# A streaming encoder trunk with mixture-of-experts layers: pairs of 1 MB weight chunks fetched in one 2 MB transfer

## What is computed

```
h = h + concat(chunk_band_attention(q, k, v), multiscale_pool(p)) @ w_out_even    # layer 0 mixer
h = h + hierarchical_moe(rms_norm(h))                                             # layer 0 experts
h = h + concat(spatial_gating(u, vv), stick_breaking_attention(q, k, v)) @ w_out_odd
h = h + hierarchical_moe(rms_norm(h))
# hierarchical_moe: each token takes 1 of 4 groups and 2 of its 8 experts;
# 32 experts, each with w_gate, w_up [1024, 256] and w_down [256, 1024]
```

## Time and profile before

| What | Value |
|---|---|
| Three runs | 591.1, 592.69, 593.89 us; median 592.69 |
| Span of the profiled execution, first to last instruction | 590.9 us |
| PE busy | 542.0 us, 92% of the span |
| DVE, ACT, POOL busy | 182.4, 180.0, 6.5 us |
| Read from memory | 234.45 MB, 399 GB/s over the span |
| SP's queue (q1) | 33328 packets, 232.07 MB, 95.2% of 16 DMA engines |
| Chain that ended last | PE 72%, DMA 21%, ACT 4%, DVE 2% |

### The profile page before, as it was taken

One profiled execution on the slowest core, in us unless ns is written; L12 is line 12 of the kernel. 1 busy time (PEld: TensorE's weight loads), 2 busy tenths in 40 slices (PEclk: granted clock), 3 DMA queues, 4 the chain that ended last, 5 costly groups with the idle time before them and its releaser, 6 DMA issues.

```text
span 590.9 us, 9379 instructions
## 1 busy us (share of the span) xinstructions
PE 542.0 (92%) x3978; PEld 339.6 (57%) x3978; DVE 182.4 (31%) x311; ACT 180.0 (30%) x341; POOL 6.5 (1%) x16
## 2 busy tenths in 40 slices
PE   6999999999999998768799999999999999986786
PEld 5788787555546544142488878875555455451533
DVE  4687845311101100010365466543111011010102
ACT  5745835111111111010384696541110111110101
POOL 0000000000000000000000000000000000000000
PEclk8999999999999999797889999999999999998979
DMA  8999999999999999999999984698999999999996
GB/s 322 421 422 419 421 420 419 422 420 422 419 419 420 420 420 422 420 421 416 420 419 420 421 361 168 262 423 349 424 420 420 420 420 422 419 420 420 421 416 240
DMA packets 34098, 236.20 MB, mean 400 GB/s; under 512 B 3777, under 2 KB 4801, under 8 KB 6017
## 3 DMA queue, kind: packets, MB, share of 16 engines
q1 hardware_dynamic: 33328, 232.07, 95.2%
q0 software_dynamic: 720, 3.45, 1.4%
HBM read 234.45 MB, written 1.05 MB: 399 GB/s over the span
## 4 chain that ended last, share of the span: by engine, by line
PE 72%; DMA 21%; ACT 4%; DVE 2%; issue 1%; SPq 0%; ACTq 0%
PE psum L1317 15%; DMA raw<-stream 15%; PE psum L1296 9%; PE psum L1345 8%; PE psum L1373 8%; PE psum L265 8%; PE psum L266 8%; PE psum L267 8%; DMA late<-stream 5%; PE psum L1388 1%; DMA xT<-x_turned 1%; ACT hid L1458 1%; PE psum L1354 1%; PE psum L523 1%; ACT whi L250 1%
## 5 line engine op out<-in xcount | busy, mean ns | idle before, releaser
L1317 PE MATMUL psum<-raw,x 128*32 128x512 f32 x680 | 91.4, 639 | 20.6 <-issue 12.0
L257 DVE TENSOR_TENSOR raw_lo<-raw,whi 128x1024 fp32r<-128x1024 f32 x52 | 62.4, 1222 | 40.8 <-ACT whi L250 40.8
L1296 PEld LDWEIGHTS psum<-pick,h 128*128 128x128 f32 x512 | 60.2, 196 | 17.3 <-issue 15.1
L1373 PE MATMUL psum<-y,pickT 128*128 128x256 f32 x256 | 69.3, 403 | 0.0
L1296 PE MATMUL psum<-pick,h 128*128 128x128 f32 x512 | 64.0, 283 | 1.0 <-DVE pick L1260 1.0
L265 PE MATMUL psum<-whi,hnT_hi 128*128 128x512 f32 x144 | 58.5, 406 | 6.0 <-DVE hnT_lo L369 3.4
L1373 PEld LDWEIGHTS psum<-y,pickT 128*128 128x128 f32 x256 | 45.5, 193 | 31.5 <-issue 27.1
L250 ACT CAST whi<-raw 128x1024 fp32r<-128x1024 f32 x52 | 53.0, 1047 | 34.2 <-PE psum L267 28.6
L1268 DVE TENSOR_TENSOR pick<-pick,lists 128x256 f32<-128x256 f32 x16 | 6.8, 425 | 179.8 <-PE psum L1388 179.8
L266 PE MATMUL psum<-whi,hnT_lo 128*128 128x512 f32 x144 | 58.0, 403 | 0.0
L267 PE MATMUL psum<-raw_lo,hnT_hi 128*128 128x512 f32 x144 | 57.8, 402 | 0.0
(11 more groups left out here) (213 smaller groups left out, 502.2 us busy)
## 6 DMA issues: line engine op xcount, KB each, us to landing
raw<-stream SPq DMA_DIRECT2D x157, 1024.0 KB, 26.7
late<-stream SPq DMA_DIRECT2D x60, 1024.0 KB, 23.0
raw<-stream SPq DMA_DIRECT2D x2, 512.0 KB, 5.6
xT<-x_turned SPq DMA_DIRECT2D x2, 512.0 KB, 6.7
h<-x SPq DMA_DIRECT2D x1, 1024.0 KB, 11.5
pb<-even_bias POOLq DMA_DIRECT2D x1, 1024.0 KB, 14.0
pool_c<-even_pool POOLq DMA_DIRECT2D x1, 1024.0 KB, 9.5
out<-h SPq DMA_DIRECT2D x4, 256.0 KB, 2.2
```

The source lines that it names most:

```text
L257: nc.vector.tensor_tensor(raw_lo[PLACE[c][0]][:, cols], chunk(c)[:, cols], whi[:, n % SPLIT, cols].bitcast(F32), ALU.subtract).then_inc(lo ...
L1296: mm = nc.tensor.matmul(psum[:, b, (k - ks[0]) * P:(k - ks[0] + 1) * P], h[:, t, k * P:(k + 1) * P], pick[:, t, :], start=(t == 0), stop=( ...
L1317: nc.tensor.matmul(psum[rows, b, :], lhs[:, rows], chunk(c)[:, e * W4:(e + 1) * W4], start=start, stop=stop).then_inc(moe_used, 1)
L1373: nc.tensor.matmul(psum[:, 4 + i, t * QUARTER:(t + 1) * QUARTER], pickT[:, t * P:(t + 1) * P], y[:, i % 2, :], start=(q == 0 and t == 0), ...
```

## The change

In the stretches named below as alone, chunks come one by one as before. Elsewhere two neighbouring chunks (an even number and the next) come in one transfer of 2 MB into two neighbouring places, and one semaphore tells of both. In memory `stream` is laid out anew: for each pair of chunks and each partition, 16 KB together; a chunk that comes alone is read with 8 KB out of each 16 KB. Alone are chunks 0 to 3, 16 to 45, 104 to 109, 126 to 155 and 214 to 217 (74 chunks); 72 pairs remain: 4 to 15, 46 to 103, 110 to 125 and 156 to 213. A pair waits for both of its places. The choice of places is made over pairs of places (0,1), (2,3) ... (14,15), (17,18) ... (23,24); place 16 stays single. In the spill path, four transfers take the place of two.

```diff
+DOUBLES = tuple((p, p + 1) for p in itertools.chain(range(0, RAW, 2), range(RAW + 1, PLACES, 2)))
+ALONE = frozenset(itertools.chain(range(0, 4), range(16, 46), range(104, 110), range(126, 156), range(214, CHUNKS)))
+def transfers():
+    found, c = [], 0
+    while c < CHUNKS:
+        together = (c,) if c in ALONE else (c, c + 1)
+        found.append(together)
+        c += len(together)
+    return tuple(found)
...
-        place = min(open_to, key=lambda p: (free[p], p))
...
+        fitting = [(p,) for p in open_to] if len(chunks) == 1 else [d for d in DOUBLES if set(d) <= set(open_to)]
+        chosen = min(fitting, key=lambda ps: (max(free[p] for p in ps), ps))
...
-        raw = [fixed(f"raw{i}", [P, CH]) for i in range(RAW)]
+        raw = [fixed(f"raw{i}", [P, 2, CH]) for i in range(RAW // 2)]
...
-        late = [at(f"late{n}", [P, CH], kib) for n, kib in enumerate(range(10, 82, 8))]
+        late_alone = at("late_alone", [P, CH], 10)
+        late = [at(f"late{n}", [P, 2, CH], kib) for n, kib in enumerate(range(18, 82, 16))]
...
+        def from_stream(c):
+            return stream[c // 2, :, c % 2, :]
...
-            sp.dma_start(chunk(c), stream[c]).then_inc(landed[place], 16)
...
+        def load_chunks(sp, chunks):
+            for c in chunks:
+                place_free(sp, c)
+            c = chunks[0]
+            if len(chunks) == 1:
+                sp.dma_start(chunk(c), from_stream(c)).then_inc(landed[PLACE[c].told_by], 16)
+            else:
+                sp.dma_start(two_places(PLACE[c].place)[:], stream[c // 2]).then_inc(landed[PLACE[c].told_by], 16)
...
-            for c in range(2, CHUNKS):
-                if c == RAW + 3:
+            for chunks in TRANSFERS[2:]:
+                if chunks[0] == RAW + 3:
                     sp.wait_ge(ev.pool_c_landed, 16)
...
-        "stream": stream,
+        "stream": np.ascontiguousarray(stream.reshape(CHUNKS // 2, 2, P, CH).transpose(0, 2, 1, 3)),
```

More of the change, by code:

```diff
@@ L96 @@
               (OUT1 - 0.9, OUT1 + 1.1, OUT1 + 1.1, OUT1 + 0.5, OUT1 + 0.5, OUT1 + 2.1, OUT1 + 3.1))
+DOUBLES = tuple((p, p + 1) for p in itertools.chain(range(0, RAW, 2), range(RAW + 1, PLACES, 2)))
[7 more added lines that the diff above has]
+    return tuple(found)
+TRANSFERS = transfers()
+Placed = namedtuple("Placed", "place told_by nth leaves")
 def places():
-    found, free, inside = [], [-1] * PLACES, [[] for _ in range(PLACES)]
-    for c in range(CHUNKS):
+    found, free, inside, told = [], [-1] * PLACES, [[] for _ in range(PLACES)], [0] * PLACES
+    for chunks in TRANSFERS:
+        c = chunks[0]
         layer = int(c >= PROJ1)
@@ L110, in places @@
         open_to = [p for p in range(PLACES) if p < RAW or is_moe(c) and (p >= RAW + TILES_IN or not last_quad)]
-        place = min(open_to, key=lambda p: (free[p], p))
[L112 to L115, removed]
+        fitting = [(p,) for p in open_to] if len(chunks) == 1 else [d for d in DOUBLES if set(d) <= set(open_to)]
+        chosen = min(fitting, key=lambda ps: (max(free[p] for p in ps), ps))
+        for c, p in zip(chunks, chosen):
+            leaves = inside[p][-1] if inside[p] and free[p] == inside[p][-1] else None
+            found.append(Placed(p, chosen[0], told[chosen[0]], leaves))
+            inside[p].append(c)
+            free[p] = c
+        told[chosen[0]] += 1
     return found
 PLACE = places()
-BEHIND = min(c for c in range(CHUNKS) if MOE0 + SPILL_AT * PER_QUAD <= (PLACE[c][2] or 0) < PROJ1)
+BEHIND = min(cs[0] for cs in TRANSFERS for c in cs if MOE0 + SPILL_AT * PER_QUAD <= (PLACE[c].leaves or 0) < PROJ1)
 C_ID, C_NTRI, C_NONE, C_LT, C_IOTA, C_EPS, C_REV = 0, 128, 256, 384, 512, 545, 546
@@ L192, in hybrid_kernel, with two_places, place_free @@
         moe_used = sem("moe_used")
+        def two_places(place):
+            return raw[place // 2] if place < RAW else late[(place - RAW - 1) // 2]
         def chunk(c):
-            place = PLACE[c][0]
-            return raw[place][:] if place < RAW else late[place - RAW][:]
-        def chunk_landed(eng, c):
[L199 to L205, removed]
+            place = PLACE[c].place
+            if place == RAW:
+                return late_alone[:]
+            return two_places(place)[:, place % 2 if place < RAW else (place - RAW - 1) % 2, :]
+        def from_stream(c):
+            return stream[c // 2, :, c % 2, :]
+        def chunk_landed(eng, c):
+            eng.wait_ge(landed[PLACE[c].told_by], 16 * (PLACE[c].nth + 1))
+        def place_free(sp, c):
+            place, leaves = PLACE[c].place, PLACE[c].leaves
+            if leaves is None:
                 if place >= RAW:
                     late_free(sp, int(c >= PROJ1), place - RAW)
-            elif is_moe(before_it):
-                sp.wait_ge(moe_used, EACH * (moe_no(before_it) + 1))
-            else:
-                sp.wait_ge(w_used, 2 * mixer_no(before_it) + 2)
-            sp.dma_start(chunk(c), stream[c]).then_inc(landed[place], 16)
+            elif is_moe(leaves):
+                sp.wait_ge(moe_used, EACH * (moe_no(leaves) + 1))
+            else:
+                sp.wait_ge(w_used, 2 * mixer_no(leaves) + 2)
+        def load_chunks(sp, chunks):
+            for c in chunks:
+                place_free(sp, c)
+            c = chunks[0]
+            if len(chunks) == 1:
+                sp.dma_start(chunk(c), from_stream(c)).then_inc(landed[PLACE[c].told_by], 16)
+            else:
+                sp.dma_start(two_places(PLACE[c].place)[:], stream[c // 2]).then_inc(landed[PLACE[c].told_by], 16)
         def late_free(sp, layer, n):
@@ L256, in split_lo @@
                 dve.wait_ge(hi_done, 2 * n + part + 1)
-                nc.vector.tensor_tensor(raw_lo[PLACE[c][0]][:, cols], chunk(c)[:, cols],
+                nc.vector.tensor_tensor(raw_lo[PLACE[c].place][:, cols], chunk(c)[:, cols],
                                         whi[:, n % SPLIT, cols].bitcast(F32), ALU.subtract).then_inc(lo_done, 1)
@@ L263, in three @@
         def three(out_ap, hi, lo, c, cols, first, last):
-            w_hi, w_lo = whi[:, mixer_no(c) % SPLIT, cols], raw_lo[PLACE[c][0]][:, cols]
+            w_hi, w_lo = whi[:, mixer_no(c) % SPLIT, cols], raw_lo[PLACE[c].place][:, cols]
             nc.tensor.matmul(out_ap, hi, w_hi, start=first, stop=False)
@@ L1513, in spill_sp @@
                     cols = slice((n % EACH) * W4, (n % EACH + 1) * W4)
[L1514 to L1517, removed]
+                    for b in range(2):
+                        gu, down = stream[c // 2:(c + GU_CHUNKS) // 2, :, b, cols], stream[(c + GU_CHUNKS) // 2:(c + PER_QUAD) // 2, :, b, cols]
+                        sp.dma_start(spill_gu[:, b:KD:2, :], gu.rearrange("a p n -> p a n")).then_inc(spl.landed, 16)
+                        sp.dma_start(spill_down[:, b:4:2, :], down.rearrange("a p n -> p a n")).then_inc(spl.landed, 16)
                 sp.wait_ge(spl.y_done, ALL)
@@ L1538, in spill_pe @@
                 for n in range(ALL):
-                    pe.wait_ge(spl.landed, 32 * (n + 1))
+                    pe.wait_ge(spl.landed, 64 * (n + 1))
                     if n:
@@ L1611, in _ @@
             sp.dma_start(cst[:], consts).then_inc(cst_landed, 16)
-            sp.dma_start(chunk(0)[:, 0:HALF_CH], stream[0, :, 0:HALF_CH]).then_inc(first_landed, 16)
+            sp.dma_start(chunk(0)[:, 0:HALF_CH], from_stream(0)[:, 0:HALF_CH]).then_inc(first_landed, 16)
             sp.dma_start(xT[:, 0:4, :], x_turned[:, 0:4, :]).then_inc(xT_landed[0], 16)
-            sp.dma_start(chunk(0)[:, HALF_CH:CH], stream[0, :, HALF_CH:CH]).then_inc(landed[0], 16)
+            sp.dma_start(chunk(0)[:, HALF_CH:CH], from_stream(0)[:, HALF_CH:CH]).then_inc(landed[0], 16)
             sp.dma_start(xT[:, 4:8, :], x_turned[:, 4:8, :]).then_inc(xT_landed[1], 16)
-            load_chunk(sp, 1)
+            load_chunks(sp, (1,))
             sp.dma_start(h[:], x_in.rearrange("a (t p) d -> p (a t) d", p=P)).then_inc(x_landed, 16)
-            for c in range(2, CHUNKS):
-                if c == RAW + 3:
+            for chunks in TRANSFERS[2:]:
+                if chunks[0] == RAW + 3:
                     sp.wait_ge(ev.pool_c_landed, 16)
-                if c == BEHIND:
+                if chunks[0] == BEHIND:
                     spill_sp(sp, 0)
-                load_chunk(sp, c)
+                load_chunks(sp, chunks)
             spill_sp(sp, 1)
```

## The result

The changed kernel took 587.9 us (median of 4, 586.97 to 589.27) against 591.9 us: a ratio of 0.9924 with the interval [0.9904, 0.9945]. By the ratio that is 4.5 us less, by the two medians 4.0. In a later series beside the same kernel before it was 0.9913 [0.9891, 0.9936]. The forecast was 591.6 us with a range down to 588.7.

The account below looks back on a forecast made before the run. DMA stream bounds up to chunk 108 and from 402 us, PE the second mixer. Gains there total 0.0 us at half clock, 2.2 at full; taking 1.1, 592.7 - 1.1 = 591.6 us, range 588.7 to 594.5.

Parts of the forecast that it names:

- I take 3.9 ns: Cost of a packet beside its bytes in a full queue; a pair saves 9 packets, 35 ns (0 to 95).
- the tail: Stretch from 402 us to the end, 29 pairs: loses 0.3 us at half clock or gains 1.0 at full.
- rival 2: A 16 KB packet is slow as such: each pair takes 3.6 us more, 230 us in all; chance 0.08.
- the middle between two clocks: PE's clock level left open between 0.0 us gain at half and 2.2 at full: 1.1 us less taken.
- the half-clock case: PE at half clock in each layer's last DMA-bound quad, whose turn starts 1.9 us later: 0.0 us gain together.
- the seam: Stretch up to chunk 108 and the first mixer cast, 35 pairs: gains 1.2 us, or 0.3 at half clock.
- The landing together: A pair's first chunk waits about 2.5 us; last DMA-bound quad's turn starts 0.9 us later, 1.9 at half clock.
- The covers: Queued work hides waits for places at pairs (46,47) and (156,157) by 3.2 and 2.3 us, pool_c's landing by 1.7.
- The rest, costed at nothing: SP's issuing, waits for places, the first mixer's pairs, POOL's queue and the unused spill path: no cost.
- Rival 1: A packet costs more, 10.5 ns: 5.9 us less in all, 586.8 us; chance 0.16.
- Rival 3: Rows are not joined, a pair stays 256 packets of 8 KB: 594.3 us at half clock; chance 0.05.
- Rival 4: A transfer's fixed cost of 2.3 us is paid each time and saved 64 times: 147 us less; chance 0.01.

Follow-up runs that it names:

- the bare stream: Kernel without any computation that only fetches the stream's bytes in stretches of different packet and transfer sizes; 2 MB landed every 4.968 us at 8 KB packets, 4.891 at 16 KB.
- either set of pairs alone: Changed kernel with pairs only up to chunk 103 (35), or only from chunk 156 (29), against the kernel before: 590.33 us (0.9967) and 590.39 us (0.9966).
- the kernel told late: Kernel before, transfers unchanged, but PE and ACT wait for both chunks where the change has pairs: 594.33 us, ratio 1.0029.

## Why the prediction was wrong

**The step that failed: "I take 3.9 ns".** The term "a pair then saves 9 x 3.9 = 35 ns" measured about 80 ns: 77 to 80 in the bare stream, 83 in the tail with pairs only there. With 64 pairs that is 5.1 us where the step had 2.2. The output's 10.5 ns, set aside because it writes, is near the 9 ns of the loads. No run here shows whether writes cost the same, so that may be luck. What misled me was the earlier trace rows: its window is 2.5 us long and holds 1.09 MB, too little for a price of some ns. I noted myself that rounding was worth 2.7 ns of the 3.9. By the time that passed, the same window gives no price at all: 40.0 us of 16 engines for bytes that take 41.7 at the pace of the earlier trace rows. So the 3.9 ns were not a measurement of the price. For the same reason "4 KB and 8 KB packets run at the same rate within 1%", said against rival 2, is wrong: in the bare stream they are 3% apart.

Busy shares are the wrong sum as well, but they err the other way. A share above 1 counts overlaps of a packet with the next, and these grow as packets shrink (102.6% at 4 KB, 101.4% at 8, 100.2% at 32). With shares the bare stream's windows would give 14 ns a packet from 4 to 8 KB instead of 10. In a full queue the time that passed is the right sum.

**The second step: the middle between two clocks.** At 3.9 ns and the full clock the prediction had 2.2 us less, and halved them to 1.1 for the half-clock case. So the factor of four is 2.3 from the price and 2 from this average, less what was lost on the way. Neither place lost anything to a late PE in the two profiled executions of the changed kernel (next paragraphs).

**What bounds the kernel** held. The gain came in the seam and in the tail, 2.0 us for either set of pairs alone.

**The landing together** held as a mechanism: the kernel told late is 1.7 us slower, against 0.7 + 1.1 = 1.8 us by the prediction's step at half clock. That the sums agree is partly luck, since its profiled execution has 2.1 us in the tail and none at the seam. In the changed kernel it is hidden. At the seam both products follow the pair's landing at half clock (0.53 from 247 to 251 us), as the step said, but PE waited again before the mixer. The timeline of the changed kernel:

```profile
247.48 3.52 PE L1357 MATMUL psum<-raw,x 128*32 128x512 f32 x16 [1.43 <-DMA raw<-stream]
250.94 3.84 PE L1336 MATMUL psum<-pick,h 128*128 128x128 f32 x32
```
```profile
285.18 1.07 PE L1385 MATMUL psum<-late,hid 128*32 128x256 f32 x16 [0.32 <-DMA late<-stream]
...
290.62 1.04 ACT L290 CAST whi<-raw 128x1024 fp32r<-128x1024 f32 x1 [0.49 <-DMA raw<-stream]
```
```profile
538.94 1.92 PE L1357 MATMUL psum<-raw,x 128*32 128x512 f32 x16 [0.86 <-DMA raw<-stream]
```
```profile
576.44 1.07 PE L1385 MATMUL psum<-raw,hid 128*32 128x256 f32 x16 [0.42 <-DMA raw<-stream]
...
578.96 1.07 PE L1385 MATMUL psum<-raw,hid 128*32 128x256 f32 x16 [0.39 <-DMA raw<-stream]
```

The gather that began at 250.25 us begins at 250.94, 0.7 us later, and the wait for DMA at the end of the layer is still there, 0.32 and 0.49 us. In the tail 16 matmuls take 1.92 us, the full clock, and PE waits 0.42 and 0.39 us for the last two chunks, as it did before. So the DMA side decided at both places, where the half-clock branch had put PE. It did so in the second profiled execution of the changed kernel too. There the clock was at half from 533 to 536 us and PE fell behind: the last pair's products were done 2.5 us after it landed (2.0 us in the first). But PE had caught up by the last chunk, for which it waited 0.39 us.

**The clock.** The two profiled executions differ by 5.7 us, 1.2 more than the ratio gives. Some 1.6 us of it are the second mixer's start at half clock in the kernel before, at 295.8 us, which neither profiled execution of the changed kernel shows: chunk 108 landed 2.2 us earlier and the places behind it came free 3.7 us earlier. Half of those 2.2 us are not the pairs' either: in the kernel before, chunk 108 landed 3.6 us after chunk 107, in the changed kernel's two executions 2.3 and 2.5 us. Of all the kept profiles only one other has both the late landing (3.6 us) and the half clock at 295.8 us: the one with pairs as two transfers. So the late chunk and the lower clock belong together; what delayed the chunk is open, and so is how often it happens. I had asked only whether the change would suffer from the lower level, not whether the kernel before did.

**The covers** that I had costed held: chunks 46 and 156 came without a gap in the queue, and pool_c delayed nothing that showed. "The rest, costed at nothing" did not hold as a whole. At 106 us the stream waits for PE to come through the first mixer (chunk 37 takes chunk 12's place), and I had worked out no cover for that. In the changed kernel PE's first product started 1.0 us later (10.58 us, before 9.61), its clock from 10 to 20 us was 0.74 instead of 0.88, and that place came free at 106.9 us instead of 105.6. The rate fell to 367 GB/s there. Chunk 15 had landed 0.7 us earlier than in the kernel before; chunk 45 landed 0.7 us later (133.3, before 132.65). At chunk 103, with all 35 pairs behind it, the stream was 1.4 us ahead, and 1.2 us in the second profiled execution, where 80 ns a pair make 2.8. The pairs are not shown to be the cause of the slow start. The kernel told late, with its transfers unchanged, has 0.73 and 387 GB/s in the same windows, and one run of the 2 MB transfers in 8 KB packets has 0.83 and 406.

**The rivals.** Rival 1 (a packet costs more) is what happened, at 9 instead of 10.5 ns; its sum gave 586.8 us, close to the 587.9 measured, though part of the stream's gain was lost at 106 us. It had 0.16 and ought to have had as much as my own case, since one row stood for each. Rival 2 (a 16 KB packet is slow as such) fell: 16 and 32 KB are faster per byte. Rival 3 fell with the packets' count. Rival 4 fell with the 2 MB transfers of 8 KB packets: no cost is seen once per transfer in a full queue. The Trainium skill's section that the prediction names with it (DMA: Bandwidth & Descriptors, "Anatomy of one DMA") is about transfers that GpSimd issues. By its figures 1 MB on an idle queue takes 4.4 us, an estimate; SP's took 4.8 us.

## What to carry to other kernels

In a stream whose queue never runs dry, a packet had a fixed price of about 9 ns on its engine and a transfer none that showed: joining rows from 8 to 16 KB gives 1.6% of the transfer-bound time, from 4 to 8 KB 3%, from 16 to 32 KB under 1%. Price it from long windows or landings, by the time that passed and not by busy shares, and where two rows give prices a factor apart, let the chance follow. Look for every stretch in which the stream waits for its places: a faster stream can run dry there and lose its gain. What it costs to have two pieces land together is paid only where the consumer has caught up, and the faster stream can pay for it.

## What was not expected of the hardware

The fixed price holds from 4 KB packets to 32 KB packets, at 8 to 10 ns each. A transfer over 64 partitions runs at half the rate, 210 against 431 GB/s with the same 16 KB packets, so each packet takes twice as long. The DMA view of that stretch, 200 to 300 us:

```profile
q1 hardware_dynamic: 1602, 21.01, 100.6%
```

The queue looks full. The Trainium skill (SBUF — State Buffer, "Door 1: The DMA port swizzle") states about 218 GB/s for 64 partitions; the trace agrees.
